# A hybrid mLSTM and attention layer on one core: four attention halves of the merge put at the end of the mLSTM stage, and one more pair of gate tiles by Strassen's scheme

## The reference

```python
u = rmsnorm(x, norm_pre_w) * (1 + scale) + shift
aq, ak, av, az, mq, mk, mv, mo, mz, mg, ga, gb = split_proj(u, w_in)
y_b = attention(aq, ak, av) * silu(az)                 # 1024 wide
y_a = head_norm(mlstm(mq, mk, mv, mg)) * sigmoid(mo) * silu(mz)   # 1024 wide, 4 heads
merged = sigmoid(ga) * (y_a @ w_proj_a) + sigmoid(gb) * (y_b @ w_proj_b)
out = rmsnorm(merged @ w_out, norm_post_w)
return x + gate * out
```

## Time and profile before

| | us |
|---|---|
| median of 3 runs | 1942.57 |
| lowest, highest | 1941.44, 1942.93 |
| the profiled execution, its own time | 1941.78 |
| its span | 1940.2 |
| TensorE busy | 1909.7 (98%) |
| VectorE busy | 1269.1 (65%) |
| ScalarE busy | 693.3 (36%) |
| POOL busy | 144.4 (7%) |
| granted clock, mean | 0.999 |

### The profile page before, as it was taken

The page is one execution under the profiler, slowest core; times in us unless marked ns, Lnnn a source line. Parts: engine busy times, 40 slices in busy tenths (PEclk is TensorE's granted clock), DMA queues, the critical chain, the costliest instruction groups (busy, mean ns, idle before and its releaser), DMA issues.

```text
span 1940.2 us, 31275 instructions
## 1 busy us (share of the span) xinstructions
PE 1909.7 (98%) x12182; PEld 1770.8 (91%) x12182; DVE 1269.1 (65%) x2181; ACT 693.3 (36%) x1077; POOL 144.4 (7%) x259
## 2 busy tenths in 40 slices
PE   6999999999999999999999999999999999999998
PEld 2589999999999999999998998899899999988886
DVE  3368877777777777887666665465466787663224
ACT  4453333333333333333555554232233443332221
POOL 2010010010001000100000000000000100000000
PEclk9999999999999999999999999999999999999999
DMA  9963464444444444544732422363552643524224
GB/s 368 391 205 88 135 190 135 135 146 135 135 135 146 130 132 133 159 143 130 205 95 88 132 82 88 98 160 120 125 138 73 208 144 104 177 76 141 77 76 163
DMA packets 299839, 278.43 MB, mean 144 GB/s; under 512 B 20976, under 2 KB 254184, under 8 KB 297824
## 3 DMA queue, kind: packets, MB, share of 16 engines
q1 hardware_dynamic: 279504, 199.93, 35.1%
q0 software_dynamic: 19936, 76.97, 11.2%
q10 hardware_dynamic: 304, 0.25, 0.0%
HBM read 237.14 MB, written 42.58 MB: 144 GB/s over the span
## 4 chain that ended last, share of the span: by engine, by line
PE 90%; DVE 4%; DMA 3%; ACT 1%; issue 1%; SPq 1%; POOL 0%; DVEq 0%; POOLq 0%; ACTq 0%
PE bank L2427 13%; PE bank L2507 12%; PE bank L2500 12%; PE bank L2501 12%; PE bank L2768 10%; PE bank L2436 7%; PE bank L2706 6%; PE bank L2710 3%; PE bank L2340 2%; PE bank L2400 2%; PE bank L2627 2%; DMA WORK<-in_w_ada_dram 2%; PE bank L2616 2%; PE bank L2568 1%; PE bank L2629 1%; PE bank L2545 1%
## 5 line engine op out<-in xcount | busy, mean ns | idle before, releaser
L1213 ACT ACTIVATE WH<-RAW 128x1024 fp32r<-128x1024 f32 x195 | 206.7, 1060 | 386.1 <-PE bank L2507 306.1
L1717 DVE TENSOR_TENSOR WL<-RAW,WH 128x1024 fp32r<-128x1024 f32 x195 | 238.4, 1223 | 68.8 <-ACT WH L1213 68.6
L2427 PE MATMUL bank<-XH,WH 128*128 128x320 f32 x1024 | 243.5, 319 | 0.9 <-issue 0.7
L1092 ACT ACTIVATE WH<-RAW 128x1024 fp32r<-128x1024 f32 x94 | 99.4, 1058 | 392.7 <-PE bank L2436 253.3
L2427 PE MATMUL bank<-XL,WH 128*128 128x320 f32 x1024 | 233.1, 309 | 0.0
L2501 PE MATMUL bank<-XL,WH 128*128 128x320 f32 x720 | 212.5, 309 | 0.0
L2500 PE MATMUL bank<-XH,WH 128*128 128x320 f32 x720 | 212.4, 309 | 0.0
L1514 DVE TENSOR_TENSOR WL<-RAW,WH 128x1024 fp32r<-128x1024 f32 x92 | 112.1, 1221 | 110.6 <-ACT WH L1092 110.4
L2427 PEld LDWEIGHTS bank<-XH,WH 128*128 128x128 f32 x1024 | 169.6, 188 | 8.7 <-issue 7.1
L2427 PEld LDWEIGHTS bank<-XL,WH 128*128 128x128 f32 x1024 | 171.3, 188 | 0.0
L2436 PE MATMUL bank<-XH,WL 128*128 128x320 f32 x1024 | 165.7, 311 | 0.3 <-DVE WL L1514 0.3
(11 more groups left out here) (279 smaller groups left out, 3626.9 us busy)
## 6 DMA issues: line engine op xcount, KB each, us to landing
RAW<-in_w_in_dram SPq DMA_DIRECT2D x165, 512.0 KB, 3.8
proj_dram<-OUTS POOLq DMA_DIRECT2D x92, 320.0 KB, 2.5
WORK<-in_w_ada_dram POOLq DMA_DIRECT2D x64, 256.0 KB, 3.6
RAW<-in_w_out_dram SPq DMA_DIRECT2D x32, 512.0 KB, 3.7
WORK<-in_w_ada_dram SPq DMA_DIRECT2D x30, 512.0 KB, 10.4
WORK<-proj_dram SPq DMA_DIRECT2D x16, 640.0 KB, 4.5
WORK<-proj_dram POOLq DMA_DIRECT2D x16, 640.0 KB, 5.4
RAW<-in_w_ada_dram SPq DMA_DIRECT2D x18, 512.0 KB, 9.3
```

Of the source, the lines that this page charges most:

```text
L1092: nc.scalar.activation(WH[:, w_slot(gs), :], RAW[:, slot, :], ACT.Copy).then_inc(hi_done, 1)
L1213: ins = nc.scalar.activation(WH[:, (j + p) % 2, :], pair_raw(j, p), ACT.Copy)
L1717: V.tensor_tensor(WL[:, w, :], pair_raw(j, p), WH[:, w, :].bitcast(F32), ALU.subtract)\
L2427: pe.matmul(banks[n][:, 0:HALF_TOK], wh[:, k, :], x[:, k0 + k, n * HALF_TOK:(n + 1) * HALF_TOK], start=(first and k == 0 and wi == 0), sto ...
```

## The change

One pair more: `PAIRS` goes from 30 to 31, and two gate tiles are computed as a pair instead of as plain tiles. The mLSTM stage keeps its 24 halves, but only 20 are gate halves (`L2_GATES` = 10 tiles); the last four, s = 20 to 23, are the attention halves n = 0..3 (`L2_MERGED` = 4). For them the last two gate tiles are interleaved (`gate_half`): both first halves (XH[0:8]), then both second halves, so that `high_y` and `low_y` for the attention outputs can be done at s = 18. The gates' loads (`gate_b`), the sigmoids and `b_gate` for n = 0..2 move into the mLSTM stage; from s = 22 on TensorE waits for `b_gated` before it takes a bank pair again. In front of the first merged pair then stand five attention halves (n = 4..8), and behind each of the seven pairs one. The quarters of WH and WL start in the other slot (`QUARTER_0`). The whole amount of work is that of before, less the difference between two plain tiles and a pair.

```diff
-T_PAIR, T_L1, T_L2, T_MERGE, T_OUT, T_END = 4, 64, 78, 90, 92, 108
+T_PAIR, T_L1, T_L2, T_MERGE, T_OUT, T_END = 4, 66, 80, 92, 94, 110
-GADA_LAST = [4, 3, 3, 3, 3]
+GADA_LAST = [3, 3, 3, 3, 2, 2]
+L2_HALVES = 24
+L2_MERGED = 4
+L2_GATES = (L2_HALVES - L2_MERGED) // 2
+T_GATES = T_L2 + L2_GATES
+LEADS = L2_MERGED + 5
+def gate_half(s):
+    t, x = divmod(s, 2)
+    if t >= L2_GATES - 2:
+        return L2_GATES - 2 + x, t - (L2_GATES - 2)
+    return t, x
-B_AFTER = [(6,), (7,), (8,), (9, 10), (11,), (12, 13), (14, 15)]
+B_AFTER = [(9,), (10,), (11,), (12,), (13,), (14,), (15,)]
...
@@ SP, mLSTM stage
-                in_tile(T_L2 + s // 2, 0, COL_MERGE + P * (GATES_PAIRED + L1_TILES + s // 2), (s % 2,))
+                if s < 2 * L2_GATES:
+                    t, x = gate_half(s)
+                    g, c = 2 * T_L2 + s, COL_MERGE + P * (GATES_PAIRED + L1_TILES + t)
+                    w_half(g - 3, g, g % 4, w_in_v[:, 8 * x:8 * x + 8, c:c + P])
+                else:
+                    g, c = 2 * T_L2 + s, P * merged_row(s - 2 * L2_GATES)
+                    w_half(g - 3, g, g % 4, w_pb_v[:, :, c:c + P])
...
@@ POOL, mLSTM stage
             for t in range(L2_TILES * M_HEADS):
                 h, k = divmod(t, L2_TILES)
+                if t == L2_GATES:
+                    pool.wait_ge(y_lo, 8)
+                if t >= L2_GATES:
+                    gate_b(t - L2_GATES)
...
-                spill(T_L2 + t, 0, RB_GA + GATES_PAIRED + L1_TILES + t)
+                if t < L2_GATES:
+                    spill(T_L2 + t, 0, RB_GA + GATES_PAIRED + L1_TILES + t)
...
@@ ScalarE, mLSTM stage
-                    if s % 2 == 0:
+                    if s % 2 == 0 and s != 2 * L2_GATES - 2 and s <= 2 * L2_GATES:
                         evac(0, T_L2 + s // 2 - 1)
+                    if s == 2 * L2_GATES - 2:
+                        act.wait_ge(yb_done, 10 * KV_HEADS + 1)
+                        act.wait_ge(w_used, 2 * T_GATES - 2)
+                        high_y(range(8), y_hi, 8)
+                    if s == 2 * L2_GATES - 1:
+                        evac(0, T_GATES - 2, 3)
+                    if s > 2 * L2_GATES and s % 2:
+                        b_sigmoid(s // 2 - L2_GATES)
...
@@ VectorE, mLSTM stage
                 if part and s + 1 < 2 * L2_TILES * M_HEADS:
                     lo(0, 0, 2 * T_L2 + s + 1)
-                if q == 4 * L2_TILES * M_HEADS - 2:
-                    low_y(range(LOW_EARLY), y_hi, y_lo, 8)
+                if q == 4 * L2_GATES - 4:
+                    low_y(range(5), y_hi, y_lo, 8)
+                if q == 4 * L2_GATES - 3:
+                    low_y(range(5, 8), y_hi, y_lo, 8)
+                if part and s > 2 * L2_GATES:
+                    b_gate(s - 2 * L2_GATES - 1)
...
@@ TensorE, mLSTM stage
+                n = s - 2 * L2_GATES
...
                 if part == 0:
-                    if x == 0:
+                    if n >= 2:
+                        pe.wait_ge(b_gated, n - 1)
+                    elif n >= 0:
+                        pe.wait_ge(out_ready, T_GATES - 1 + n)
+                        pe.wait_ge(y_lo, 8)
+                    elif x == 0:
                         pe.wait_ge(out_ready, t - 1)
...
@@ TensorE, merge
-            for n in range(6):
+            for n in range(L2_MERGED, LEADS):
                 b_product(n)
```

More of the change, by code:

```diff
@@ L1003, in head_rows, with gate_b, gate_a @@
                 return proj[bass.ds(2 * P * h + rb * P, 2 * P), :].rearrange("(c p) t -> p c t", p=P)
+            def gate_b(k):
+                row = merged_row(2 * k)
+                if k:
+                    pool.wait_ge(sig_in[0], 16 * k)
+                for t in range(T_L2 + row + 2 - GATES_PAIRED, T_L2 + row + 4 - GATES_PAIRED):
+                    if t >= T_L2:
+                        pool.wait_ge(spilled[t % 2], 16 * (t // 2 + 1))
+                pool.dma_start(y_pair(k), proj[(RB_GB + row) * P:(RB_GB + row + 2) * P, :]
+                               .rearrange("(c p) t -> p c t", p=P)).then_inc(sig_in[0], 16)
+            def gate_a(a):
+                row = merged_row(2 * a)
+                if a:
+                    pool.wait_ge(sig_in[1], 16 * a)
+                pool.dma_start(MTB[a % 2], proj[(RB_GA + row) * P:(RB_GA + row + 2) * P, :]
+                               .rearrange("(c p) t -> p c t", p=P)).then_inc(sig_in[1], 16)
             for t in range(L2_TILES * M_HEADS):
                 h, k = divmod(t, L2_TILES)
+                if t == L2_GATES:
+                    pool.wait_ge(y_lo, 8)
+                if t >= L2_GATES:
+                    gate_b(t - L2_GATES)
                 if k == 1:
@@ L1426, in _ @@
             high_y(range(8, 12), y_hi, 8)
[L1427 removed]
+            b_hi(L2_MERGED + 2)
             high_y(range(12, KT), y_hi, 8)
[L1429 to L1430 removed]
+            for k in range(L2_MERGED // 2, 3):
+                b_sigmoid(k)
+            b_hi(L2_MERGED + 3)
             ta_high(0)
             ta_high(1)
[L1433 to L1435 removed]
+            b_sigmoid(3)
+            b_hi(L2_MERGED + 4)
             ta_high(2)
             ta_high(3)
[L1438 removed]
             for a in range(MERGES):
@@ L2041, in statistics, with b_gate @@
                 V.tensor_scalar(MVAR[:, :, 1], MVAR[:, :, 1], EPS, None, ALU.add).then_inc(ml_var, 1)
+            def b_gate(n):
+                if n < L2_MERGED + 2:
+                    dve.wait_ge(w_used, 2 * T_GATES + n + 1)
+                else:
+                    dve.wait_ge(p_used, USED_0 + B_UNIT[n] + 2)
+                dve.wait_ge(sig_done, sigmoid_b(n // 2))
+                for h in range(2):
+                    at = Y[:, merged_row(n), h * HALF_TOK:(h + 1) * HALF_TOK]
+                    ins = V.tensor_tensor(at, b_bank(n)[h][:, 0:HALF_TOK], at, ALU.mult)
+                ins.then_inc(b_gated, 1)
             for q in range(4 * L2_TILES * M_HEADS):
@@ L2114, in b_lo @@
                                 ALU.subtract).then_inc(p_lo, 1)
[L2116 to L2121, removed]
-                dve.wait_ge(sig_done, sigmoid_b(n // 2))
-                for h in range(2):
-                    at = Y[:, merged_row(n), h * HALF_TOK:(h + 1) * HALF_TOK]
-                    ins = V.tensor_tensor(at, b_bank(n)[h][:, 0:HALF_TOK], at, ALU.mult)
-                ins.then_inc(b_gated, 1)
             def ta_sum(n):
@@ L2197, in half_gate @@
                 V.tensor_tensor(y, y, gate, ALU.add).then_inc(merged, 1)
-            low_y(range(LOW_EARLY, 8), y_hi, y_lo, 8)
             lo(0, 0, 2 * T_MERGE)
+            b_gate(L2_MERGED - 1)
             lo(0, 0, 2 * T_MERGE + 1)
@@ L2256, in _ @@
                     b_lo(n, 1)
-            b_gate(14)
             lo(0, 0, 2 * T_MERGE + 2)
@@ L2660, in _ @@
                 s, part = divmod(q, 2)
-                t, x = T_L2 + s // 2, s % 2
-                banks, w = bank[2 * (t % 2):2 * (t % 2) + 2], w_slot(2 * t + x)
+                t, x = gate_half(s)
+                t, g = t + T_L2, 2 * T_L2 + s
+                n = s - 2 * L2_GATES
+                banks, w = bank[2 * (t % 2):2 * (t % 2) + 2], w_slot(g)
+                k0, first, last = 8 * x, x == 0, x == 1
+                if n >= 0:
+                    banks, k0, first, last = bank[2 * (n % 2):2 * (n % 2) + 2], 0, True, True
                 for h, r in phases(q):
@@ L2693, in _ @@
                 if part == 0:
-                    high_products(banks, w, 8 * x, range(4, 6), x == 0)
+                    high_products(banks, w, k0, range(4, 6), first)
                 else:
-                    low_products(banks, w, 8 * x, x == 1, range(4, 8)).then_inc(w_used, 1)
+                    low_products(banks, w, k0, last, range(4, 8)).then_inc(w_used, 1)
             def unit(u, terms):
```

135 lines of the change are left out of this document (57 added, 78 removed).

## The result

| | before | after |
|---|---|---|
| median, us | 1942.57 | 1945.38 |
| ratio, with its 95% interval | | 1.0015 (1.0009 to 1.0021) |
| the profiled execution, its own time | 1941.78 | 1946.45 |
| its span | 1940.2 | 1944.3 |
| TensorE's matmuls | 12182 | 12158 |

A forecast was written before the change was run, and what follows sets the result against it. TensorE, busy in 98% of the span, was taken as the bound: number of matmuls times spacing. Terms -3.5 - 1.9 + 4.4 + 0.8 = -0.2 us took the median from 1942.57 to 1942.4, range 1939.5 to 1946.3.

The forecast's parts named there:

- The pair: One more pair in place of two plain gate tiles: 24 matmuls less on TensorE, -3.5 us.
- The old border: First attention half behind the mLSTM stage: its late start and waits for low parts go, -1.9 us.
- The copies moved into head 3: ScalarE's eight row copies in the middle of head 3, covered by idle times of ScalarE and VectorE: nothing added.
- Half 22 behind `b_gate(0)`: In the mLSTM stage TensorE waits for the first gate, late in VectorE's order: +4.4 us, bounds 0 and 5.5.
- The second gate: `b_gate(1)` in front of half 23: no second wait, with 0.5 us to spare.
- The clock: Granted clock behind the new wait in front of half 22: the forecast assumed no fall and added nothing.
- the rivals: Cases against the forecast: clock falls in the new wait, 0.30; more waits, 0.14; gate not in the way, 0.11.
- the rival's price: Cost if the granted clock falls in the new wait: 2.1 us, between 0 and 4.2, giving 1944.5; chance 0.30.
- the reasons against the fall: Head 3 runs dense on both sides of the gap, and a fall may differ between executions; no size given.
- The end of the merge: First half of the last projection waits for its weights, landing in 7.9 us: +0.8 us, bounds 0 and 2.5.

## Why the prediction was wrong, step by step

- **The pair, -3.5.** Right. There are 24 matmuls less, and the 29 pairs from 206.71 to 920.89 us take 24.63 us each, as in the earlier trace rows (line L2528, which was L2500).

```profile
206.71:920.89 714.18, 479.17 (x1625) 304.87 (x1625) 1.00 0.47 141
```

- **The old border, -1.9.** Right, with -2.0 measured: from half 23 to the first attention half behind the stage and on to the next 8.13 and 7.04 us (1518.97, 1527.10, 1534.14), where the earlier trace rows have 8.53 and 8.64. But the term and the wait are not independent. The wait before it gives the same slack: the kernel before with the wait and without the change got the 2.0 us too. With the gates early, 0.5 us of it come back (8.52 and 7.14), until the third gate is moved.
- **The copies moved into head 3, 0.** Right: from the stage's first half to half 20 it is 233.5 us in both kernels, and half 20 to half 21 takes 22.48 in both.
- **Half 22 behind `b_gate(0)`, +4.4.** Right, in place and size: half 21 to half 22 takes 13.32 us instead of 8.95, 4.37 more. The second gate didn't hold half 23. The bound put on it (if the first comes early, the second takes all but 0.5 us of the gain) was measured as 2.95 us.
- **The clock: the step that failed.** The forecast put the clock's term at nothing: its sum has the wait of 4.4 us and no price for what comes behind it. The mechanism stood among the rivals with a chance of 0.30. The runs showed a fall in all three traces of kernels with the wait of 4.2 us unfilled, at a price of 1.65, 2.4 and 2.6 us. That the rival's price, 2.1, is so near is in part luck, as it was the middle between 0 and 4.2. What misled was the weight given to the reasons against the fall. The prediction says that the new wait "is longer than the shortest idling behind which it fell", yet it forecast none. The earlier trace rows show one instance, 3.03 us of idling at 1.00 and 0.50 after that; in the runs 2.8 and once 2.1 us were enough, and 3.4 us twice were not. And "head 3 runs dense on both sides of the gap" was an argument with no row behind it: the clock fell there. The Trainium skill, "TensorE: Matmul & The Clock Gate", section "HAM oscillation — how this bites in real kernels", says that waits between bursts of matmuls throttle the engine again, so that each next burst starts at the low rate. The traces agree in the main, with 0.50 behind 11 of the 14 waits, not behind each.
- **The end of the merge, +0.8.** Right in place and releaser, too small: +1.5 in this trace, and a named wait of 1.0 to 1.5 us in all the others that keep POOL's loads early. The term that was mis-sized is the landing, 8.6 us instead of the 7.9 carried over from before; it is within the bound of 2.5. It is the second mis-sized term, by 0.7 us; without the clock's fall the sum would be +0.5.
- **Not forecast.** The attention stage took 293.7 us, 1.7 more than before, of which 1.2 are the wait for the rotated keys. VectorE makes them late because it waits 4.4 us for a load, where it waited 2.7 before:

```profile
960.48 0.69 DVE L1896 TENSOR_TENSOR Y<-Y,WORK 128x512 f32<-128x512 f32 x1 [4.39 <-DMA WORK<-proj_dram]
```

The nine traced executions of the changed kernel and its variants have 292.4 to 293.7 us, mean 293.0, with 0 to 1.2 us of the wait for the rotated keys, and each takes 292.4 to 292.6 us plus that wait. The four of the kernel before and its variants have 292.0 to 292.8, mean 292.4. Most of the 1.7 is thus scatter of when loads land; whether 0.6 of it belongs to the change is open. The +0.4 us ahead of the second pair is scatter as well: over the same executions the attention stage begins 24.4 us later on average, no more than the new pair's 24.63.

By medians the parts close, with the unforecast ones left out: -3.5 - 1.9 + 4.4 + 1.5 and 1.65 to 2.6 for the clock are +2.1 to +3.1, measured +2.8. And with both waits gone, -3.5 - 1.9 + 0.5 = -4.9, measured 1937.65 - 1942.57 = -4.9. That the second agrees to the tenth is in part luck, since the interval reaches 2 us to each side.

## What to carry to other kernels

A new wait of TensorE in a dense stretch costs its length and may cost the granted clock behind it as well. Here a wait of 4.2 us cost 1.65 to 2.6 us more in each of three traces, and waits of 3.4 us did so in seven of nine: put that into the sum itself when the wait is that long, not among the rivals. When a result is passed to another engine to free a bank, look for the earliest place in that engine's order at which its inputs are there: the gate ran 12.4 us behind the start of half 21 and could run 1.6 us behind it, and this one condition was worth 6.5 us, more than the 5.4 that the pair and the border bring. And two terms next to each other on the path (a wait, and a stall just behind it) are not to be added without asking whether the first gives the second its slack.

## What the runs showed of the hardware

The granted clock can fall while TensorE still idles (it is 0.50 from 1505.9 on in one execution, with half 22 starting at 1507.55) or only as it starts again (0.50 from 1509.6 on, half 22 at 1509.42). The first kind costs more, 2.4 to 2.6 us in its three cases against 1.5 to 1.65 us in the nine of the second; 0.1 us of each is lost behind such a wait at 1.00 too. I had not expected that a longer stretch at 1.2 GHz would lie behind the same wait in the same kernel. Nor that a stretch of matmuls in the wait, as small as 12 of 192 columns (1.5 us), would go with a clock that holds through the remaining 2.9 us. That is a single execution beside a single traced fall behind 2.8 us, and the wait of 2.8 us seems to leave the clock up in half of its executions without any matmuls in it. So it is no more than a hint.
